# Layer zero of a two-block transformer kernel: the gated mlp's spatial product moved behind the second gate, its end behind the third

## What is computed

```
p = h @ w_in[l]
y_att  = dilated_mixture_attention(q, k, v)
y_rwkv = rwkv7_time_mix(p[..., i0:i1], ...)
y_gmlp = chunked_spatial_gating(p[..., i1:i2], ln_g, ln_b, w_s, b_s)
gates  = sigmoid(p[..., i2:])                     # three gates, 1024 columns each
branch = einsum('bsnw,nwd->bsnd', stack([y_att, y_rwkv, y_gmlp]), w_branch[l])
merged = sum(gates * branch, axis=2)

def chunked_spatial_gating(p_uv, ln_g, ln_b, w_s, b_s):
    z = gelu(p_uv)                                # u, v = the two halves
    v = layer_norm(v, ln_g, ln_b)                 # "token norm" in the kernel
    s = einsum('gij,bcjgd->bcigd', tril(w_s), v) + b_s   # "spatial"
    return u * s                                  # "gmlp y" splits it for the next product
```

## Time and profile before

| | us |
|---|---|
| median of 3 runs | 2110.16 |
| lowest and highest | 2108.58, 2110.57 |
| the profiled execution | 2109.37 |
| its span in the profile | 2107.4 |
| PE busy in it | 2090.7 (99%) |
| DVE busy in it | 1638.5 (78%) |

### The profile page before, as it was taken

How to read it: one execution, slowest core, us unless ns; L and a number is a source line. 1 busy time by engine, 2 the same in 40 slices (tenths; PEclk the granted TensorE clock), 3 DMA queues, 4 the chain that set the end, 5 groups by cost and what they waited for, 6 DMA issues and landing times.

```text
span 2107.4 us, 39168 instructions
## 1 busy us (share of the span) xinstructions
PE 2090.7 (99%) x16342; PEld 1900.9 (90%) x16342; DVE 1638.5 (78%) x2520; ACT 1235.3 (59%) x2007; POOL 13.4 (1%) x20
## 2 busy tenths in 40 slices
PE   8999999999999999999999999999999999999999
PEld 7898999999998899998888989888898888998888
DVE  7899788887887788877887657787688765788876
ACT  4755756555756655555665448665475644766654
POOL 0000000000000000000000000000000000000000
PEclk9999999999999999999999999999999999999999
DMA  9566567768645467655555754555555557455554
GB/s 372 200 215 217 173 222 253 247 229 283 228 155 176 163 209 233 216 185 189 183 191 188 232 158 160 203 189 190 188 181 189 190 196 224 139 176 206 190 190 130
DMA packets 122114, 424.57 MB, mean 201 GB/s; under 512 B 13465, under 2 KB 22041, under 8 KB 121170
## 3 DMA queue, kind: packets, MB, share of 16 engines
q1 hardware_dynamic: 121938, 422.08, 59.9%
HBM read 417.68 MB, written 4.35 MB: 200 GB/s over the span
## 4 chain that ended last, share of the span: by engine, by line
PE 92%; DVE 4%; ACT 1%; DMA 1%; issue 0%; SPq 0%; POOL 0%; ACTq 0%; DVEq 0%
PE bank L208 92%; DVE arena L214 2%; DVE lo L214 1%; DMA raw<-W 1%; ACT arena L259 1%; PE bank L211 1%; DVE arena L222 1%; ACT hi L259 0%; DVE ada L231 0%; DMA xT<-x 0%; DVE arena L218 0%; SPq L205 0%; POOL arena L214 0%; ACT L251 0%; DVE sml L240 0%
## 5 line engine op out<-in xcount | busy, mean ns | idle before, releaser
L208 PE MATMUL bank<-h,hi 128*128 128x256 f32 (+1 forms) x5248 | 1183.2, 312 | 0.0
L259 ACT ACTIVATE hi<-raw 128x1024 fp32r<-128x1024 f32 x656 | 689.0, 1057 | 525.5 <-PE bank L208 454.8
L208 PE MATMUL bank<-h,lo 128*128 128x256 f32 x3328 | 949.1, 285 | 0.0
L208 PEld LDWEIGHTS bank<-h,hi 128*128 128x128 f32 x5248 | 861.4, 190 | 60.3 <-issue 1.9
L214 DVE TENSOR_TENSOR lo<-raw,hi 128x1024 fp32r<-128x1024 f32 x656 | 792.2, 1221 | 96.7 <-ACT hi L259 95.8
L208 PEld LDWEIGHTS bank<-h,lo 128*128 128x128 f32 x3328 | 633.7, 190 | 11.7 <-issue 7.8
L208 PE MATMUL bank<-act,hi 128*128 128x512 f32 x1056 | 370.0, 393 | 0.0
L208 PE MATMUL bank<-act,lo 128*128 128x256 f32 x1056 | 294.7, 279 | 0.0
L208 PEld LDWEIGHTS bank<-act,hi 128*128 128x128 f32 x1056 | 197.9, 187 | 47.0
L208 PEld LDWEIGHTS bank<-act,lo 128*128 128x128 f32 x1056 | 197.9, 187 | 0.0
L259 ACT ACTIVATE arena<-arena 128x256 f32<-128x256 f32 (+4 forms) x202 | 98.6, 493 | 158.9 <-DVE arena L214 151.4
(11 more groups left out here) (152 smaller groups left out, 1941.2 us busy)
## 6 DMA issues: line engine op xcount, KB each, us to landing
raw<-W SPq DMA_DIRECT2D x664, 512.0 KB, 4.1
ada<-WA SPq DMA_DIRECT2D x80, 512.0 KB, 3.8
arena<-WA SPq DMA_DIRECT2D x16, 512.0 KB, 13.9
arena<-conv_rows SPq DMA_DIRECT2D x16, 280.0 KB, 6.3
arena<-taps SPq DMA_DIRECT2D x2, 1792.0 KB, 7.9
p_projected<-arena SPq DMA_DIRECT2D x2, 1024.0 KB, 7.3
arena<-p_projected SPq DMA_DIRECT2D x2, 1024.0 KB, 4.8
arena<-scr SPq DMA_DIRECT2D x10, 128.0 KB, 4.9
```

The costliest lines, as they stand in the source:

```text
L208: return self.done(lambda e: e.matmul(out, l, r, start=start, stop=stop, skip_group_check=True))
L259: return self.done(lambda e: e.activation(out, in_, f, scale=scale, **kw))
```

## The change

```diff
@@ main_order, for each layer l @@
         s += [("gmlp v", l), ("token norm", l), ("gmlp u", l, 0), ("gmlp u", l, 1), ("gate", l, 2, 0),
-              ("until", ("ln", l)), ("spatial", l), ("gate", l, 2, 1), ("gmlp y", l), ("flag", ("gmlp", l)),
-              ("pause", False), ("gate", l, 2, 2), ("gate", l, 2, 3), ("until", ("prep", l))]
+              *[("gate", l, 2, 1)] * (1 - l), ("until", ("ln", l)), ("spatial", l), ("gate", l, 2, 2 - l), ("gmlp y", l), ("flag", ("gmlp", l)),
+              ("pause", False), *[("gate", l, 2, 2)] * l, ("gate", l, 2, 3), ("until", ("prep", l))]
```

## The result

| | before | after |
|---|---|---|
| median, us | 2110.19 (4 runs) | 2120.32 (4 runs) |
| lowest and highest | 2108.58, 2110.57 | 2119.15, 2121.91 |
| profiled execution | 2109.37 | 2119.15 |
| its span | 2107.4 | 2117.1 |

The ratio is 1.005, with a 95% interval from 1.0039 to 1.0062: slower by 10.1 us, where the forecast was +1.5 us and the range ended at 2114.9. Of the cases named, it lies where E did, 2119 to 2121, but not for E's reason, as will be seen.

The account below looks back on a forecast made before the run. PE, busy 99%, was taken to bound the kernel, with DVE full in the changed stretch. +1.76 down to block 26, -0.35 at "inv0" and +0.1 at the scores gave +1.5 us, 2111.7, range 2108.6 to 2114.9.

Parts of the forecast that it names:

- E: Rival: the clock falls at "bonus sum" and stays low down to block 29, about 9 us, 2119 to 2121; 7%.
- The waits that go, and the one that comes: Around block 24: spatial's waits of 1.90 and 0.28 us go; PE waits 4.13 us for DVE at "bonus sum".
- Down to block 26: From "bonus sum" to block 26: a 0.20 us wait goes too, and block 26 starts at 113.74, +1.76 us.
- inv0: PE step behind block 29, waiting for DVE's "level0": its 0.40 us wait goes, priced -0.35; start about 128.8 us.
- Later: Effects further on: scores' bank waits, recurrence's end and modulation columns, priced +0.1, 0 and 0 us.
- +0.1 at the scores: Waits behind attention's scores, 191 to 198 us: "x" 1 waits for a second bank readout; 0 to +0.3 us.
- The clock: Behind the 4.13 us wait: a possible fall to half rate, priced at +2.3 us, not in the main sum.
- B: Rival: the clock falls for one stretch behind the long wait, +3.8 us, from 2.8 to 4.8; 13%.
- C: Rival: neither spatial nor "bonus sum" waits, -2.8 us, 2107.4; 6%.
- D: Rival: later stretches give it back as waits at 124.47 and 191 to 198 vanish; +0.4 us, -0.5 to 0.6; 16%.

Follow-up runs that it names:

- e1: Kernel before with only spatial moved behind gate quarter 1 in layer zero, gmlp y, flag and pause end staying in time: 2116.15 us, ratio 1.0027.
- e3: Changed kernel with the attention's scores one tick later too in layer zero: 2115.24 us, ratio 1.0030.
- e6: Changed kernel with scores one tick later and 24 unread filler matmuls ahead of "bonus sum": 2114.21 us, ratio 1.0022.
- e9: Changed kernel with 24 unread filler matmuls ahead of "bonus sum" alone: 2117.53 us, ratio 1.0035.
- e5: Kernel before with one empty tick added to layer zero's recurrence between "unit" 0 and "level0" 0, nothing else: 2115.55 us, ratio 1.0026.
- e4: Changed kernel with 24 unread filler matmuls ahead of "bonus sum" and 24 ahead of "x" 1: 2115.29 us, ratio 1.0027.
- e12: Changed kernel with "x" 1 and "inv0" 1 put ahead of "scores" 0 within the same tick of layer zero: 2115.22 us, ratio 1.0024.
- e2: Kernel before with spatial left in place and gmlp y, the flag and the pause's end moved behind gate quarter 2: 2115.98 us, ratio 1.0026.
- e8: Kernel before with spatial behind gate 1, recurrence on time, modulation one quarter later, "cross" 0 0 ahead of "bonus sum": 2110.76 us, ratio 1.0005.
- e7: Changed kernel with scores one tick later and "cross" 0 0 exchanged with "bonus sum" in layer zero: 2112.05 us, ratio 1.0010.

## Why the prediction was wrong

**The waits that go, and the one that comes: right.** No wait is left ahead of block 24 or spatial, and one wait stands at "bonus sum" for L222. It was 2.97 us, not 4.13, since PE was 0.9 late there, 0.77 of it from before the change, and "bonus" was done 0.3 early. E1 and e3, with 3.50 and 3.91, show how it varies.

**Down to block 26, and "inv0": 0.8 us too low, since the clock was left out.** The forecast put "inv0" at 128.80 us, and it came at 129.61, +2.17 in place of +1.4. The clock cost 1.69. Most of the rest went the other way: the wait ended at 104.52 and not at 104.76, "cross" 0 0 and spatial took 3.83 us and not 4.31, and block 26 to "inv0" 14.90 and not 15.06, together 0.88 less. That the sum missed by no more than 0.8 is in part luck. E6 and e9, without that fall, came out 1.0 and 1.5 us lower. "Inv0" had no wait and ysl did wait for ysh (1.58), as said.

**"Later", the term "+0.1 at the scores": this is the step that failed.** It measured 5.5 us in the profile. I had written that the recurrence is one tick later, and then priced only one more bank to be read out. DVE's readout at its old time was right (190.53 in e5, 190.62 before). What was wrong is that PE, too, was left coming to it at its old time: its "x" 1 and "inv0" 1 (2.74 us in e4's rows) no longer stood ahead of "scores" 0 but behind. The wait grew by 2.74 us, and the clock, which fell in it, cost 2.87 more. It is the very mechanism that I had worked out at "bonus sum": PE loses its cover and comes to DVE early. E5 shows that the tick alone does it and that PE's side moved, e3 and e12 that the order against the scores is what matters. The 0.8 for ACT at "u12" belongs to the same omission: in e2 and e5 it is there with the late recurrence, in e8, where the recurrence is on time, it isn't. I had followed the recurrence past the scores on DVE alone and not on ACT's queue.

**The clock: B's mechanism was right and its chance too small.** It fell behind the first long wait, at 1.7 us rather than the 2.3 that I took from the earlier trace rows. I gave a fall 20% in all, B and E together, with "against it that PE had been at work without a gap for tens of us before", and the clock fell all the same. It then fell a second time, behind a wait that the forecast didn't have. E, a clock that stays low down to block 29, didn't happen: from block 26 to "inv0" it took 14.90 us (114.71 to 129.61), where the forecast, at the full clock, had 15.06. The rule of the Trainium skill, "TensorE: Matmul & The Clock Gate", section "HAM oscillation — how this bites in real kernels", that an idle gap brings PE back to half rate and its next work starts slowly, agrees with the windows of 0.50 behind the waits of 2.97 and 3.53 us. What would have helped is to weigh the rule as the likely case.

**C and D fell.** DVE was the full engine, as said, and nothing was given back: the waits behind the scores grew.

**The range** ended 5.4 us under the time that was measured because the largest term had been put at 0 to +0.3, with no case for it. The bound of 0.2% was passed by 5.5 us at the scores and 0.8 at "u12"; without these the time would by these rows have been within it.

## What to carry to other kernels

When a change delays a chain of side work by one step, list every place further on where that chain meets another one, and redo there the sum that was made at the place of the change: which work of the busiest engine stood ahead of its wait, and doesn't any more. Then take the length of each wait that comes out: here one of 3 us of PE cost half its length again or more (1.69 us behind 2.97, 2.87 behind 3.53), since the clock was at half behind it, and filling it with work, even with useless work (e4), took that part away; waits of 1.2 and 0.4 us in its place (e7) left the clock alone.

## What the runs showed of the hardware that I had not expected

- The granted clock goes down in the middle of a program that has kept PE busy 99% of its time. It was at 0.50 in every profile behind a wait of 2.97 to 3.91 us (after, e1, e2, e3, e5, and e9 to e12), and in none behind waits of 1.65 (before), 1.48 (e2), 1.35 (e3, e6) or 1.22 (e7). The one between, 1.78 us in e1, was followed by a window of 0.50 too, some 20 us behind that kernel's first fall. Not counted are the waits of the program's first 14 us, 3.4 us ahead of PE's first matmul and 2.9 ahead of 13.78: the granted clock reads 1.00 behind both in every profile, though the matmuls come slowly there. What the clock was there is not shown.
- It falls in the wait or close behind it. In e1 it was 0.86 from 102 to 103 us, in e5 0.85 from 190 to 191, inside waits that ended at 103.82 and 191.42.
- The same wait is followed by unequal slow stretches. Behind 3.52 or 3.53 us at "x" 1 it was 6.9 us in after (0.51 over 7.00), and in e9 and e2 3.4 us (0.57 over 4.00 in e9). E5, whose wait was 3.52 too, was like after, with 6.9 us (0.57 over 8.00):

```profile
190.00:198.00 8.00, 6.58 (x89) 6.26 (x90) 5.41 (x9) 1.42 (x4) 0.00 (x0) 0.57 0.55 194
```

- It isn't in every execution: one of e1's six had a mean granted clock of 1.000 and was 3.4 us faster than the next, the same kernel on the same chip.
